# RG-LRU/HGRN2 blocks: the lambda constant, the weight splits and the row scale put elsewhere

## The chip, the cores and the metric

The kernel runs on one core of one Trainium2 chip. The metric is the device time of one execution in microseconds, as the median of several runs. Names of engines: TensorE (PE in the profile, PEld for its weight loads), VectorE (DVE), ScalarE (ACT), GpSimd (POOL), SyncE (SP, which issues the DMAs).

## The reference

A decoder trunk of two layers, 1024 tokens, width 1024, all in float32. Each layer normalises its input, projects it with one matrix w_in, and gives the columns to four head groups: A latent attention, B an RG-LRU recurrence, C stick-breaking attention, D an HGRN2 gated recurrence. Their outputs go through one projection, then a SwiGLU follows. This case concerns groups B and D:

```python
# B: RG-LRU
xc = depthwise_conv4(xb) + conv_b
rec_gate = sigmoid(blockdiag(xc, w_a) + b_a); in_gate = sigmoid(blockdiag(xc, w_x) + b_x)
log_a = -8.0 * rec_gate * softplus(-lam)
a = exp(log_a); u = sqrt(maximum(-expm1(2 * log_a), 0)) * (in_gate * xc)
y = scan(h = a * h + u) * gelu(gate)
# D: HGRN2
log_f = logaddexp(log(max(lb, 1e-30)), log1p(-lb) + log_sigmoid(fz)); key = (1 - lb) * sigmoid(-fz)
o = gated recurrence over chunks (q, key, v, log_f)
y = rmsnorm(o) * silu(g)
```

## The kernel before

Everything is kept with features on the 128 partitions and the 1024 tokens along the row. The input scale of the norm (RS, one value for each token) is not applied to the activations; each projected tile is multiplied by RS when it is read out of PSUM. A matrix product in near-full float32 is done as three products of two halves: every weight tile is split into w_hi and w_lo (w_lo = raw - w_hi), and so are the activations (u_hi, u_lo). `product` runs over eight k, and for each k three pairs of 128x512 matmuls (L217).

`group_bd` is one block and runs four times: for two layers, two pairs of heads each. Between blocks stands a barrier of all engines. In a block, eight weight tiles ("slots") of 128x1024 pass through two buffers (even and odd). Slot 1 is the q weights, slot 2 g, slot 3 v, slot 4 the conv input x, slot 5 the gate; slots 0 and 1 of a block were loaded and split ahead of it, and slots 6 and 7 are those of the next stage. SyncE loads slot n when slot n-2 is split; GpSimd splits slot n (`split_slot`, L200 w_hi and L203 w_lo) when the product of slot n-2 has ended, and multiplies g, v and gate by RS (L593) after ScalarE has copied them from PSUM (L734, L737, L742).

The order of the work on each engine is written out by hand. VectorE starts with the constants of the pair: copies L773 and L775, and then the softplus of -lambda as a chain of one-column steps (L789 to L800). Then comes f from PSUM (L802), with ScalarE's Abs, Exp and Ln in turns, the cumulative sum (L818), and `level_in(0)`, `level_in(1)`. Then q is scaled out of PSUM (L881), which frees pair 1 for slot 3. The loop over seven levels follows: `level_keys(L)` (L844, L846), `level_scores(L-1)` (two L861, which wait for the level's last chunk on TensorE), `level_in(L+2)` (L832, L833), and at L = 4 `conv` (L868 to L875). TensorE does the levels' small matmuls (L605) inside the slot products: level 0 inside slot 3 (its last chunk ahead of k = 7), levels 1 and 2 inside slot 4, levels 3 and 4 inside slot 5, level 5 behind it, and level 6 between the matmuls of the gates w_a and w_x (L648). The gates want pair 1 of PSUM free, which the read of gate does.

PSUM is used in four pairs of banks; `bank_free[p]` counts the reads that free pair p.

Of the kernel before, what the change touches and what calls it, by code (L numbers as in the profile page):

```python
# [26 lines left out]
F32 = mybir.dt.float32  # L27
# [40 lines left out]
W_LBA, W_LBC, W_LBD, W_C1, W_T0, W_T1, W_T2, W_T3, W_T4, W_N = 9, 10, 11, 12, 13, 14, 15, 16, 17, 18  # L68
# [11 lines left out]
def build(nc, x, positions, vec_table, w_in, w_uq, w_ukv, w_a, w_x, lb_logits, w_out,  # L80
# [5 lines left out]
    with ctx:  # L86
# [15 lines left out]
        lbt = fixed("lower_bound", [P, 3, 4])  # L102
# [197 lines left out]
        LW = at_r("lb_work", 73, [P, 12, 4])  # L300
        PI_ = at_r("pos_int", 76, [1, S], I32)
# [13 lines left out]
        lb_step = sem("lb_step")  # L315
        with nc.Block() as block:
# [26 lines left out]
            def _(dve):  # L343
# [3 lines left out]
                dve.wait_ge(small_loaded, 80)  # L347
# [55 lines left out]

                dve.wait_ge(x_rs, 2)
# [10 lines left out]
            def _(act):  # L415
                act.wait_ge(lb_step, 3)
# [33 lines left out]
            def _(pe):  # L450
                pe.wait_ge(small_loaded, 80)
# [51 lines left out]
        lam_part = sem("lam_part")  # L503
# [33 lines left out]
        gelu_part = sem("gelu_part")  # L537
        pool_scaled = sem("pool_scaled")
# [3 lines left out]
        la_ready = sem("la_ready")  # L542
# [9 lines left out]
        def group_bd(l, pr):  # L552
# [8 lines left out]
            with nc.Block() as block:  # L561
# [18 lines left out]
                @block.gpsimd  # L580
                def _(pool):

                    nc.gpsimd.memset(SC[:, :, :, :], 0.0).then_inc(sc_zero, 1)
                    nc.gpsimd.memset(ST[:, :, :], 0.0).then_inc(st_zero, 1)
                    nc.gpsimd.memset(XP[:, 0:3], 0.0).then_inc(st_zero, 1)

                    for n in range(2, len(slots) + 2):
                        split_slot(pool, n, n // 2, n - 2)
                        if n in (4, 5, 7):
                            t, (read, count) = {4: (bG, (bank_free[0], 2)), 5: (bV, (bank_free[1], 2)),  # L590
                                                7: (GT, (bank_free[1], 3))}[n]
                            pool.wait_ge(read, count)
                            nc.gpsimd.tensor_tensor(t[:, :], t[:, :], RS[:, :], ALU.mult).then_inc(pool_scaled, 1)  # L593

                @block.tensor
                def _(pe):
# [39 lines left out]
                    pe.wait_ge(pool_scaled, 2)  # L636
# [67 lines left out]
                def _(act):  # L704
                    exp_and_ln()

                    act.wait_ge(pair_vecs, 2)
                    nc.scalar.activation(col(W_T0), col(V_LAM), ACT.Abs).then_inc(lam_part, 1)
                    act.wait_ge(lam_part, 1)
                    nc.scalar.activation(col(W_T0), col(W_T0), ACT.Exp, scale=-1.0).then_inc(lam_part, 1)  # L710
# [6 lines left out]
                    nc.scalar.activation(bT[:, :], bT[:, :], ACT.Ln, bias=1.0).then_inc(f_soft, 1)  # L717

# [8 lines left out]
                    act.wait_ge(cum_ready, NCH)  # L727
                    nc.scalar.activation(EC[:, :], bCUM[:, :], ACT.Exp).then_inc(ec_ready, 1)
# [12 lines left out]
                    act.wait_ge(proj_done, 5)  # L741
                    nc.scalar.activation(wide(GT[:, :]), pair(1), ACT.Copy).then_inc(bank_free[1], 1)  # L742
# [6 lines left out]
                    act.wait_ge(pool_scaled, 3)  # L749
                    nc.scalar.activation(GE[:, :], GT[:, :], ACT.Square).then_inc(gelu_sq, 1)  # L750
                    nc.scalar.activation(XP[:, 0:S], bG[:, :], ACT.Sigmoid).then_inc(silu_th, 1)
                    act.wait_ge(gelu_in, 1)
                    nc.scalar.activation(GE[:, :], GE[:, :], ACT.Sigmoid, scale=2 * math.sqrt(2 / math.pi))\
                        .then_inc(gelu_th, 1)
                    act.wait_ge(la_ready, 1)
                    act.wait_ge(level_done, LEVELS)
                    nc.scalar.activation(TH[:, :], TR[:, :], ACT.Tanh).then_inc(decay_ready, 1)
                    exp_and_ln()
                    act.wait_ge(dve_step, 1)
                    nc.scalar.activation(XP[:, 0:S], TR[:, :], ACT.Exp).then_inc(decay_ready, 1)  # L760
# [7 lines left out]
                    act.wait_ge(neg_ready, 1)  # L768
                    nc.scalar.activation(TH[:, :], TH[:, :], ACT.Sqrt).then_inc(root_ready, 1)

                @block.vector
                def _(dve):
                    nc.vector.tensor_copy(pv[:, 0:PAIR_ROWS], vecs[:, bass.ds(pr * PAIR_ROWS, PAIR_ROWS)])\  # L773
                        .then_inc(pair_vecs, 1)
                    nc.vector.tensor_copy(pv[:, W_LBA:W_LBA + 3].rearrange("p (i o) -> p i o", o=1),  # L775
                                          lbt[:, :, bass.ds(l * 2 + pr, 1)]).then_inc(pair_vecs, 1)
                    dve.wait_ge(pair_vecs, 2)


                    n = 2  # L780

                    def step(ins):
                        nonlocal n
                        n += 1
                        ins.then_inc(pair_vecs, 1)
                        dve.wait_ge(pair_vecs, n)

                    nc_ts = nc.vector.tensor_scalar
                    step(nc_ts(col(W_T1), col(V_LAM), -1.0, 0.0, ALU.mult, ALU.max))  # L789
                    dve.wait_ge(lam_part, 2)  # L790
                    step(nc_ts(col(W_T2), col(W_T0), 2.0, None, ALU.add))
                    step(nc.vector.reciprocal(col(W_T2), col(W_T2)))
                    step(nc.vector.tensor_tensor(col(W_T2), col(W_T2), col(W_T0), ALU.mult))
                    step(nc.vector.tensor_tensor(col(W_T3), col(W_T2), col(W_T2), ALU.mult))
                    step(nc_ts(col(W_T4), col(W_T3), 1.0 / 17, 1.0 / 15, ALU.mult, ALU.add))
                    for term in (13, 11, 9, 7, 5, 3, 1):
                        step(nc_ts(col(W_T4), col(W_T4), col(W_T3), 1.0 / term, ALU.mult, ALU.add))
                    step(nc.vector.tensor_tensor(col(W_T4), col(W_T4), col(W_T2), ALU.mult))
                    step(nc.vector.scalar_tensor_tensor(col(W_T4), col(W_T4), 2.0, col(W_T1), ALU.mult, ALU.add))
# [83 lines left out]
                    for L in range(LEVELS):  # L883
# [3 lines left out]
                        if L + 2 < LEVELS:  # L887
                            level_in(L + 2)
# [1148 lines left out]
```

## Time and profile before

| what | value |
|---|---|
| median of 3 runs | 3028.69 us (3024.24 to 3029.8) |
| profiled execution, span | 3029.8 us, the value of the slowest of the three runs too |
| TensorE busy | 2841.3 us, 94% |
| VectorE / ScalarE / GpSimd busy | 1501.9 / 735.0 / 1143.6 us |
| mean granted TensorE clock | 0.949 of full speed |
| the four blocks of `group_bd` | from 49, 181, about 1524 and 1655 us, 122 to 132 us each |

The span is cut by barriers: setup up to 49 us, and in each layer two blocks of `group_bd`, the latents, attention and the feed-forward part. Busy time that overlaps a busier engine costs nothing by itself; what counts are the waits of the engine that is last in each stretch.

### The profile page before, as it was taken

To read this page: it belongs to the slowest core of one execution; us is meant where nothing else is said; L and a number is where in the kernel's file an instruction comes from. 1 tells how busy PE (TensorE), PEld (TensorE's weight loads), DVE (VectorE), ACT (ScalarE), POOL (GpSimd) and SP (SyncE) were. 2 spreads that over 40 slices of the span, in tenths; PEclk is the share of its full clock that TensorE was granted. 3 is DMA by queue.
4 is the path that set the end of the run, shared out by engine and by line. 5 is a ranking of instruction groups with operands and counts; after the bars stand their busy time and mean duration, and the time that the engine had idled before them with its cause. 6 is when DMAs were issued, how large, how long until landed. Compare 5 with 4: busy or idle time off the path is not lost. (4 is left out here: it accounts for less than half of the span.)

```text
span 3029.8 us, 33194 instructions
## 1 busy us (share of the span) xinstructions
PE 2841.3 (94%) x13112; PEld 2217.0 (73%) x13112; DVE 1501.9 (50%) x1745; ACT 735.0 (24%) x980; POOL 1143.6 (38%) x522
## 2 busy tenths in 40 slices
PE   7898989879999999999988899889799999999997
PEld 5666767567788888888866667566578888888886
DVE  6778248773323333332668853678522333333336
ACT  5233136562100000000223221656411000000003
POOL 3332332125544443344532323222265434434434
PEclk8899989789999999999999989788899999999999
DMA  4010210011211111111110011000212111111113
GB/s 160 15 35 8 56 25 1 0 70 36 63 49 55 56 42 48 42 42 55 70 44 21 22 29 45 8 1 0 77 49 77 47 43 42 42 48 59 52 35 111
DMA packets 201198, 134.53 MB, mean 44 GB/s; under 512 B 29346, under 2 KB 189218, under 8 KB 201123
## 3 DMA queue, kind: packets, MB, share of 16 engines
q1 hardware_dynamic: 201122, 133.49, 14.4%
q8 instruction: 51, 0.84, 0.1%
q14 instruction: 25, 0.20, 0.0%
HBM read 116.69 MB, written 16.78 MB: 44 GB/s over the span
## 5 line engine op out<-in xcount | busy, mean ns | idle before, releaser
L217 PE MATMUL ps<-u_hi,w_hi 128*128 128x512 f32 x2384 | 770.6, 405 | 58.2 <-DVE q L881 21.2
L217 PE MATMUL ps<-u_lo,w_hi 128*128 128x512 f32 x2384 | 753.7, 397 | 0.0
L217 PE MATMUL ps<-u_hi,w_lo 128*128 128x512 f32 x2384 | 753.1, 397 | 0.0
L217 PEld LDWEIGHTS ps<-u_hi,w_hi 128*128 128x128 f32 x2384 | 445.4, 190 | 172.1 <-issue 38.8
L217 PEld LDWEIGHTS ps<-u_lo,w_hi 128*128 128x128 f32 x2384 | 453.5, 190 | 106.8
L217 PEld LDWEIGHTS ps<-u_hi,w_lo 128*128 128x128 f32 x2384 | 453.1, 190 | 106.5
L1591 POOL TENSOR_TENSOR w_hi<-w_raw,ones 128x1024 fp32r<-128x1024 f32 x88 | 166.7, 1894 | 441.0 <-PE ps L217 436.5
L200 POOL TENSOR_TENSOR w_hi<-w_raw,ones 128x1024 fp32r<-128x1024 f32 (+1 forms) x62 | 118.9, 1918 | 512.9 <-PE ps L217 411.9
L1663 DVE TENSOR_TENSOR h<-ps,h 128x1024 f32<-128x1024 f32 x176 | 211.3, 1218 | 149.1 <-PE ps L217 149.1
L1648 DVE TENSOR_TENSOR hidden<-ps,hidden 128x1024 f32<-128x1024 f32 x44 | 53.9, 1225 | 434.3 <-PE ps L217 434.3
L1594 POOL TENSOR_TENSOR w_lo<-w_raw,w_hi 128x1024 fp32r<-128x1024 f32 x88 | 251.0, 2852 | 6.9
L1631 ACT ACTIVATE hidden<-hidden 128x1024 f32<-128x1024 f32 x44 | 46.7, 1061 | 740.8 <-DVE hidden L1644 740.8
L1444 POOL TENSOR_TENSOR sb_weight<-sb_z,sb_weight 128x256 f32<-128x256 f32 (+7 forms) x64 | 89.9, 1404 | 348.6 <-DVE sb_weight L1410 348.6
L1644 DVE TENSOR_TENSOR hidden<-ps,rs 128x1024 f32<-128x1024 f32 x44 | 53.9, 1224 | 314.0 <-PE ps L217 295.6
L1601 POOL TENSOR_TENSOR down_hi<-down_raw,ones 128x1024 fp32r<-128x1024 f32 x40 | 77.7, 1943 | 320.5 <-DVE h L1663 320.5
L217 PE MATMUL ps<-hidden_hi,down_hi 128*128 128x512 f32 x640 | 197.2, 389 | 0.0
L217 PE MATMUL ps<-hidden_hi,down_lo 128*128 128x512 f32 x640 | 197.2, 389 | 0.0
L217 PE MATMUL ps<-hidden_lo,down_hi 128*128 128x512 f32 x640 | 197.1, 389 | 0.0
L203 POOL TENSOR_TENSOR w_lo<-w_raw,w_hi 128x1024 fp32r<-128x1024 f32 (+1 forms) x62 | 171.2, 2761 | 4.9
L1635 ACT ACTIVATE hidden_hi<-hidden 128x1024 fp32r<-128x1024 f32 x44 | 46.8, 1063 | 518.8 <-DVE hidden L1651 518.8
L217 PEld LDWEIGHTS ps<-hidden_hi,down_hi 128*128 128x128 f32 x640 | 120.1, 188 | 25.2
L217 PEld LDWEIGHTS ps<-hidden_lo,down_hi 128*128 128x128 f32 x640 | 120.1, 188 | 25.1
(307 smaller groups left out, 3623.4 us busy)
## 6 DMA issues: line engine op xcount, KB each, us to landing
w_raw<-w_in SPq DMA_DIRECT2D x44, 512.0 KB, 3.8
w_raw<-w_gate SPq DMA_DIRECT2D x44, 512.0 KB, 3.7
w_raw<-w_up SPq DMA_DIRECT2D x44, 512.0 KB, 3.8
down_raw<-w_down SPq DMA_DIRECT2D x44, 512.0 KB, 5.1
h_spill<-h SPq DMA_DIRECT2D x24, 512.0 KB, 2.6
w_raw<-w_out SPq DMA_DIRECT2D x16, 512.0 KB, 3.4
h<-h_spill SPq DMA_DIRECT2D x16, 512.0 KB, 6.8
x_in<-x SPq DMA_DIRECT2D x8, 512.0 KB, 7.1
```

Of the source, the lines that this page charges most:

```text
L200: nc.gpsimd.tensor_tensor(whi[i][:, 0:width], raw[i][:, 0:width], ones[:, 0:1].broadcast_to([P, width]), ALU.mult).then_inc(hi_split, 1)
L203: nc.gpsimd.tensor_tensor(wlo[i][:, 0:width], raw[i][:, 0:width], whi[i][:, 0:width].bitcast(F32), ALU.subtract).then_inc(slot_split, 1)
L217: last = nc.tensor.matmul(ps[:, bank0 + half, :], a, b[:, half * HALF:(half + 1) * HALF], start=(k == order[0] and n == 0), stop=(k == ord ...
L1444: nc.gpsimd.tensor_tensor(RW[i % 2][:, 0:n], ZS[i % 2][:, 0:n], RW[i % 2][:, 0:n], ALU.subtract).then_inc(lw_ready, 1)
L1591: nc.gpsimd.tensor_tensor(whi[q % 2][:, :], raw[q % 2][:, :], ones[:, 0:1].broadcast_to([P, 1024]), ALU.mult).then_inc(hi_split, 1)
L1594: nc.gpsimd.tensor_tensor(wlo[q % 2][:, :], raw[q % 2][:, :], whi[q % 2][:, :].bitcast(F32), ALU.subtract).then_inc(slot_split, 1)
L1601: nc.gpsimd.tensor_tensor(DHI[t][:, :], DRAW[t][:, :], ones[:, 0:1].broadcast_to([P, 1024]), ALU.mult).then_inc(down_hi, 1)
L1631: nc.scalar.activation(HT[t][:, :], HT[t][:, :], ACT.Silu).then_inc(silu_done, 1)
L1635: nc.scalar.activation(HIDH[b][:, t, :], HT[t][:, :], ACT.Copy).then_inc(hid_hi, 1)
L1644: nc.vector.tensor_tensor(wide(HT[t][:, :]), pair(pg), wide(RS[:, :]), ALU.mult)\
L1648: nc.vector.tensor_tensor(wide(HT[t][:, :]), pair(pu), wide(HT[t][:, :]), ALU.mult)\
L1663: nc.vector.tensor_tensor(wide(h[:, m, :]), pair(p), wide(h[:, m, :]), ALU.add)\
```

## The change

Four things are done, nearly all in `group_bd`:

1. The constant -8 softplus(-lambda) is computed once in setup for both layers and pairs (a new DMA of 2 KB, two ScalarE and 23 VectorE instructions of 4 columns), and stored as a fourth row of `lbt`. A block copies the constants on ScalarE.
2. `split_slot` on GpSimd is gone from the block: `slot_hi` on ScalarE and `slot_lo` on VectorE take its place, each at a place in its engine's order.
3. The reads of g, v and gate from PSUM are VectorE multiplications by RS; ScalarE's copies and GpSimd's multiplications are gone.
4. Around the decay and gelu: the multiplication of rec_gate by the constant goes into the `scale` of Tanh and Exp, the square of the decay goes to ScalarE, gelu's scale and product are one instruction, and the maximum with zero is a Relu on ScalarE ahead of Sqrt.

```diff
 # setup, @block.sync
+    sp.dma_start(LV[:, 0, :], lam[:, :]).then_inc(small_loaded, 16)
...
 # setup, @block.vector, behind the angles and ahead of the wait on x_rs
+    dve.wait_ge(lam_soft, 2)
+    lam_next(nc.vector.tensor_scalar(v(5), v(0), -1.0, 0.0, ALU.mult, ALU.max))
...
+    for term in (13, 11, 9, 7, 5, 3, 1):
+        lam_next(nc.vector.tensor_tensor(v(4), v(4), v(3), ALU.mult))
+        lam_next(nc.vector.tensor_scalar(v(4), v(4), 1.0 / term, None, ALU.add))
...
+    lam_next(nc.vector.tensor_scalar(lbt[:, 3, :], v(4), -LRU_C, None, ALU.mult))
...
 # group_bd
 @block.scalar
+    def slot_hi(n):
+        i = n % 2
+        act.wait_ge(raw_loaded[i], 16 * (n // 2))
+        if n > 2:
+            act.wait_ge(proj_done, n - 2)
+        nc.scalar.activation(whi[i][:, :], raw[i][:, :], ACT.Copy).then_inc(hi_split, 1)
...
+    slot_hi(2)        # behind the first Ln
...
+    slot_hi(3)        # behind key
     for L in range(LEVELS):
         act.wait_ge(e_in, 2 * (L + 1))
         nc.scalar.activation(LE[L % 2][:, :], LE[L % 2][:, :], ACT.Exp).then_inc(e_ready, 1)
-        if L == 1:
-            act.wait_ge(proj_done, 2)
-            nc.scalar.activation(wide(bG[:, :]), pair(0), ACT.Copy).then_inc(bank_free[0], 1)
-        if L == 3:
-            act.wait_ge(proj_done, 3)
-            nc.scalar.activation(wide(bV[:, :]), pair(1), ACT.Copy).then_inc(bank_free[1], 1)
+        if L in (1, 3, 5):
+            slot_hi({1: 4, 3: 5, 5: 6}[L])
...
-    act.wait_ge(proj_done, 5)
-    nc.scalar.activation(wide(GT[:, :]), pair(1), ACT.Copy).then_inc(bank_free[1], 1)
...
+    nc.scalar.activation(XC[:, :], XP[:, 0:S], ACT.Square).then_inc(decay_sq, 1)
+    slot_hi(7)
...
     act.wait_ge(neg_ready, 1)
+    nc.scalar.activation(TH[:, :], TH[:, :], ACT.Relu, scale=-1.0).then_inc(root_ready, 1)
+    act.wait_ge(root_ready, 1)
     nc.scalar.activation(TH[:, :], TH[:, :], ACT.Sqrt).then_inc(root_ready, 1)

 @block.vector
+    def slot_lo(n):
+        i = n % 2
+        dve.wait_ge(hi_split, n - 1)
+        nc.vector.tensor_tensor(wlo[i][:, :], raw[i][:, :], whi[i][:, :].bitcast(F32),
+                                ALU.subtract).then_inc(slot_split, 1)
-    step(nc_ts(col(W_T1), col(V_LAM), -1.0, 0.0, ALU.mult, ALU.max))
...
-    step(nc_ts(col(W_C1), col(W_T4), -LRU_C, None, ALU.mult))
...
     nc.vector.tensor_scalar(bM[:, :], bB[:, :], col(W_LBC), col(W_LBA), ALU.add, ALU.max)
     dve.wait_ge(logf_ready, 1)
+    slot_lo(2)
...
     nc.vector.tensor_tensor(wide(bQ[:, :]), pair(1), wide(RS[:, :]), ALU.mult).then_inc(bank_free[1], 1)
+    slot_lo(3)
     for L in range(LEVELS):
         level_keys(L)
         if L >= 1:
             level_scores(L - 1)
         if L + 2 < LEVELS:
             level_in(L + 2)
+        if L == 1:
+            dve.wait_ge(proj_done, 2)
+            nc.vector.tensor_tensor(wide(bG[:, :]), pair(0), wide(RS[:, :]), ALU.mult).then_inc(bank_free[0], 1)
+            slot_lo(4)
+        if L == 3:
+            dve.wait_ge(proj_done, 3)
+            nc.vector.tensor_tensor(wide(bV[:, :]), pair(1), wide(RS[:, :]), ALU.mult).then_inc(bank_free[1], 1)
+            slot_lo(5)
         if L == 4:
             conv()
+        if L == 5:
+            slot_lo(6)
     nc.vector.tensor_tensor(chunks(bF), ..., ALU.subtract).then_inc(kx2_ready, 1)
+    dve.wait_ge(proj_done, 5)
+    nc.vector.tensor_tensor(wide(GT[:, :]), pair(1), wide(RS[:, :]), ALU.mult).then_inc(bank_free[1], 1)
...
+    slot_lo(7)        # behind y_d, ahead of the product with the root
     dve.wait_ge(root_ready, 2)
     nc.vector.tensor_tensor(TI[:, :], TI[:, :], TH[:, :], ALU.mult).then_inc(dve_step, 1)

 @block.gpsimd
-    for n in range(2, len(slots) + 2):
-        split_slot(pool, n, n // 2, n - 2)
-        if n in (4, 5, 7):
...
-            nc.gpsimd.tensor_tensor(t[:, :], t[:, :], RS[:, :], ALU.mult).then_inc(pool_scaled, 1)

 @block.tensor
-    pe.wait_ge(pool_scaled, 2)
+    pe.wait_ge(bank_free[1], 2)
```

## Rows read from the trace of the kernel before

**Rows 1.** The page: busy time, share and instructions of each engine.
```profile
PE 2841.3 (94%) x13112; PEld 2217.0 (73%) x13112; DVE 1501.9 (50%) x1745; ACT 735.0 (24%) x980; POOL 1143.6 (38%) x522
```

**Rows 2.** The page's costliest groups: busy, mean | idle before, releaser.
```profile
L217 PE MATMUL ps<-u_hi,w_hi 128*128 128x512 f32 x2384 | 770.6, 405 | 58.2 <-DVE q L881 21.2
```

**Rows 3.** Timeline of TensorE, first block: start, us, instruction [idle before <-releaser].
```profile
81.28 1.22 PE L217 MATMUL ps<-u_hi,w_hi 128*128 128x512 f32 x2 [7.56 <-DVE q L881]
...
98.15 0.66 PE L605 MATMUL ps<-q_level,log_f 64*128 64x64 f32 x8
...
115.76 0.66 PE L605 MATMUL ps<-q_level,log_f 64*128 64x64 f32 x8
...
133.19 2.00 PE L605 MATMUL ps<-q_level,log_f 64*128 64x64 f32 x32
...
138.34 2.38 PE L648 MATMUL ps<-x_conv,w_a_blocks 128*128 128x512 f32 x4 [2.12 <-ACT gate L742]
...
142.12 2.07 PE L648 MATMUL ps<-x_conv,w_x_blocks 128*128 128x512 f32 x2
...
147.60 1.12 PE L605 MATMUL ps<-q_level,log_sig 64*128 64x64 f32 x8
```

**Rows 4.** Timeline of VectorE, start of the first block.
```profile
55.95 1.71 DVE L797 TENSOR_SCALAR pair_vectors<-pair_vectors 128x1 f32<-128x1 f32 x7
...
58.63 1.22 DVE L802 TENSOR_TENSOR f<-ps,rs 128x1024 f32<-128x1024 f32 x1
...
80.01 1.21 DVE L881 TENSOR_TENSOR q<-ps,rs 128x1024 f32<-128x1024 f32 x1
```

**Rows 5.** Timeline of ScalarE, first block.
```profile
59.88 1.06 ACT L713 ACTIVATE soft<-f 128x1024 f32<-128x1024 f32 x1 [7.18 <-DVE f L802]
```

**Rows 6.** Timeline of VectorE, two instructions of level_keys.
```profile
103.61 3.40 DVE L846 TENSOR_TENSOR log_sig<-key,f 128x1024 f32<-128x1024 f32 x1
...
109.94 1.23 DVE L846 TENSOR_TENSOR log_f<-key,soft 128x1024 f32<-128x1024 f32 x1
```

**Rows 7.** Timeline of GpSimd, one multiplication by RS.
```profile
103.10 2.83 POOL L593 TENSOR_TENSOR v<-v,rs 128x1024 f32<-128x1024 f32 x1
```

**Rows 8.** Timeline of VectorE, first block, 96 to 175 us.
```profile
96.68 1.35 DVE L861 COPY_PREDICATED scores<-level_mask,ps 128x512 f32<-128x512 uint8 x2 [8.41 <-PE ps L605]
...
122.97 1.31 DVE L861 COPY_PREDICATED scores<-level_mask,ps 128x512 f32<-128x512 uint8 x2 [0.52 <-PE ps L605]
...
133.05 1.30 DVE L861 COPY_PREDICATED scores<-level_mask,ps 128x512 f32<-128x512 uint8 x2
...
138.96 2.45 DVE L861 COPY_PREDICATED scores<-level_mask,ps 128x512 f32<-128x512 uint8 x2
141.21 1.25 DVE L895 TENSOR_TENSOR f<-cum 128x1024 f32<-128x1024 f32 x1
...
174.29 1.22 DVE L962 TENSOR_TENSOR in_gate<-in_gate,tanh_log_a 128x1024 f32<-128x1024 f32 x1
```

**Rows 9.** Timeline of VectorE in setup.
```profile
29.36 1.23 DVE L405 TENSOR_TENSOR rs_diagonal<-x_mean_sq,constants 128x1024 f32<-128x1024 f32 x1 [3.49 <-ACT x_mean_sq L435]
30.51 9.65 DVE L267 SCALAR_TENSOR_TENSOR u_lo<-h,vectors,u_hi 128x1024 fp32r<-128x1024 f32 x8
```

**Rows 10.** Timeline of TensorE, start of slot 3 in the second block.
```profile
206.99 0.72 PE L217 MATMUL ps<-u_hi,w_hi 128*128 128x512 f32 x2 [1.90 <-DVE q L881]
...
211.52 0.66 PE L605 MATMUL ps<-q_level,log_sig 64*128 64x64 f32 x8
```

**Rows 11.** Timeline of TensorE, gate phase of the second block.
```profile
263.88 1.96 PE L648 MATMUL ps<-x_conv,w_a_blocks 128*128 128x512 f32 x4 [2.12 <-ACT gate L742]
...
269.51 0.66 PE L605 MATMUL ps<-q_level,log_sig 64*128 64x64 f32 x8
```

**Rows 12.** Windows of the third block: busy of each engine, PEclk, DMA share, GB/s.
```profile
1615.00:1617.00 2.00, 2.00 (x6) 0.50 (x5) 2.00 (x3) 0.00 (x0) 1.52 (x1) 0.50 0.00 0
...
1619.00:1621.00 2.00, 2.00 (x17) 1.18 (x18) 1.11 (x1) 1.14 (x2) 0.00 (x0) 1.00 0.00 0
```

More of the change, by code:

```diff
@@ L77, with build @@
 PI_BELOW = 3.1415925
-def build(nc, x, positions, vec_table, w_in, w_uq, w_ukv, w_a, w_x, lb_logits, w_out,
+def build(nc, x, positions, vec_table, w_in, w_uq, w_ukv, w_a, w_x, lb_logits, lam, w_out,
           w_gate, w_up, w_down, consts, level_masks, out):
@@ L101, in build @@
         vecs = fixed("vectors", [P, V_ROWS])
-        lbt = fixed("lower_bound", [P, 3, 4])
+        lbt = fixed("lower_bound", [P, 4, 4])
         pv = fixed("pair_vectors", [P, W_N])
@@ L300, in build @@
         LW = at_r("lb_work", 73, [P, 12, 4])
+        LV = at_r("lam_work", 74, [P, 6, 4])
         PI_ = at_r("pos_int", 76, [1, S], I32)
@@ L315, in build @@
         lb_step = sem("lb_step")
+        lam_soft = sem("lam_soft")
+        lam_step = sem("lam_step")
         with nc.Block() as block:
@@ L402, in _, with lam_next @@
                 turn(nc.vector.tensor_scalar(AN[:, :], AN[:, :], PI_BELOW, -PI_BELOW, ALU.min, ALU.max))
+                c = 0
+                def lam_next(ins):
+                    nonlocal c
+                    c += 1
+                    ins.then_inc(lam_step, 1)
+                    dve.wait_ge(lam_step, c)
+                v = lambda i: LV[:, i, :]
+                dve.wait_ge(lam_soft, 2)
+                lam_next(nc.vector.tensor_scalar(v(5), v(0), -1.0, 0.0, ALU.mult, ALU.max))
+                lam_next(nc.vector.tensor_scalar(v(2), v(1), 2.0, None, ALU.add))
+                lam_next(nc.vector.reciprocal(v(2), v(2)))
+                lam_next(nc.vector.tensor_tensor(v(2), v(2), v(1), ALU.mult))
+                lam_next(nc.vector.tensor_tensor(v(3), v(2), v(2), ALU.mult))
+                lam_next(nc.vector.tensor_scalar(v(4), v(3), 1.0 / 17, 1.0 / 15, ALU.mult, ALU.add))
+                for term in (13, 11, 9, 7, 5, 3, 1):
+                    lam_next(nc.vector.tensor_tensor(v(4), v(4), v(3), ALU.mult))
+                    lam_next(nc.vector.tensor_scalar(v(4), v(4), 1.0 / term, None, ALU.add))
+                lam_next(nc.vector.tensor_tensor(v(4), v(4), v(2), ALU.mult))
+                lam_next(nc.vector.scalar_tensor_tensor(v(4), v(4), 2.0, v(5), ALU.mult, ALU.add))
+                lam_next(nc.vector.tensor_scalar(lbt[:, 3, :], v(4), -LRU_C, None, ALU.mult))
                 dve.wait_ge(x_rs, 2)
@@ L415, in _ @@
             def _(act):
+                act.wait_ge(small_loaded, 96)
+                nc.scalar.activation(LV[:, 1, :], LV[:, 0, :], ACT.Abs).then_inc(lam_soft, 1)
+                act.wait_ge(lam_soft, 1)
+                nc.scalar.activation(LV[:, 1, :], LV[:, 1, :], ACT.Exp, scale=-1.0).then_inc(lam_soft, 1)
                 act.wait_ge(lb_step, 3)
@@ L704, in _ @@
                 def _(act):
+                    def slot_hi(n):
[4 more added lines that the diff above has]
+                        nc.scalar.activation(whi[i][:, :], raw[i][:, :], ACT.Copy).then_inc(hi_split, 1)
                     exp_and_ln()
+                    nc.scalar.activation(pv[:, 0:PAIR_ROWS], vecs[:, bass.ds(pr * PAIR_ROWS, PAIR_ROWS)], ACT.Copy)\
+                        .then_inc(pair_vecs, 1)
+                    nc.scalar.activation(pv[:, W_LBA:W_LBA + 4].rearrange("p (i o) -> p i o", o=1),
+                                         lbt[:, :, bass.ds(l * 2 + pr, 1)], ACT.Copy).then_inc(pair_vecs, 1)
                     act.wait_ge(pair_vecs, 2)
-                    nc.scalar.activation(col(W_T0), col(V_LAM), ACT.Abs).then_inc(lam_part, 1)
-                    act.wait_ge(lam_part, 1)
-                    nc.scalar.activation(col(W_T0), col(W_T0), ACT.Exp, scale=-1.0).then_inc(lam_part, 1)
                     act.wait_ge(bank_free[0], 1)
@@ L888, in _ @@
                             level_in(L + 2)
+                        if L == 1:
+                            dve.wait_ge(proj_done, 2)
+                            nc.vector.tensor_tensor(wide(bG[:, :]), pair(0), wide(RS[:, :]), ALU.mult)\
+                                .then_inc(bank_free[0], 1)
+                            slot_lo(4)
+                        if L == 3:
+                            dve.wait_ge(proj_done, 3)
+                            nc.vector.tensor_tensor(wide(bV[:, :]), pair(1), wide(RS[:, :]), ALU.mult)\
+                                .then_inc(bank_free[1], 1)
+                            slot_lo(5)
                         if L == 4:
                             conv()
+                        if L == 5:
+                            slot_lo(6)
                     cum = chunks(bCUM)
@@ L896, in _ @@
                                             ALU.subtract).then_inc(kx2_ready, 1)
+                    dve.wait_ge(proj_done, 5)
+                    nc.vector.tensor_tensor(wide(GT[:, :]), pair(1), wide(RS[:, :]), ALU.mult)\
+                        .then_inc(bank_free[1], 1)
                     dve.wait_ge(ec_ready, 1)
```

83 lines of the change are left out of this document (27 added, 56 removed).

## The prediction, made before the changed kernel was timed

> **What bounds the kernel now.** I read the page first: TensorE is busy 94% of the span, VectorE half of it, GpSimd 38% [rows 1]. So only work that makes TensorE wait is worth time. The costliest group of instructions shows where it waits: of 58.2 us of idle time ahead of the first product of a slot, 21.2 us end with one VectorE instruction, the scaling of q at L881 [rows 2]. From then on I read the first of the four recurrence blocks (49 to 181 us) in order of time, VectorE and ScalarE beside TensorE, then the second (181 to 303 us). In the first, TensorE waits 7.6 us for q, runs three slot products behind each other without a wait (slot 3 from 81.28, slot 4 from 98.15, slot 5 from 115.76 to 133.19), then waits 2.1 us for ScalarE's gate copy, and from 133 us on it shares the path with VectorE [rows 3]. The same pattern stands in all four blocks; only the q wait differs (1.9 us in the second).
>
> **The start of a block.** Today VectorE first works out the lambda constant: steps of 0.2 us each, 7 of them 1.71 us [rows 4], and scales f at 58.63, 9 us after the start; q is scaled at 80.01. In the changed kernel f is scaled at once; ScalarE starts its Abs some 2 us after the block's start (a table load of 1.3 and two copies of 0.2), at 51.4 instead of 59.88 [rows 5]. Between this Abs and the end of q lie 21.3 us today, of which VectorE lost about 7 to GpSimd: an L846 with a GpSimd multiplication beside it takes 3.40, one alone 1.23 [rows 6, 7], and this stretch has four such instructions, slowed by 1.3 to 2.1 each. With GpSimd's splits gone and none of the new instructions on the chain (ScalarE's split of slot 2 fits before its second Abs, VectorE's while ScalarE does its second softplus), q is done at about 51.4 + 21.3 - 7 = 66, and slot 3 is split at 68. TensorE ends slot 2 at 73.6 by its own work. All the waits on q go: 21.2 us. With the wait goes what it does to the clock: slot 3 takes 16.9 us (81.28 to 98.15); slot 5 takes 17.4 with eight level chunks more, at 0.66 for two [rows 3], so slot 3 would be 14.8 at full clock. That is 2.1, taken as 2.0 in each block. Term: -21.2 - 8.0 = **-29.2**. The cover for the moved work is 5.5 us of slack (68 against 73.6); if it were gone, each us late costs one per block.
>
> **The reads of g and v, and the splits of slots 4 and 5.** Before, ScalarE and GpSimd did these early, in their own queues. Now they stand in VectorE's queue behind level_scores(0) and level_in(3), and for slot 5 behind level_scores(2) and level_in(5). level_scores can't start before the last chunk of a level, and that chunk is issued with the last k of the slot product: L861 starts at 96.68 and slot 4 at 98.15 [rows 3, 8]; slot 5 shows the same 1.5, as do the other blocks. So VectorE begins 1.5 us before TensorE wants the next slot, and then has to do the two score copies (1.2), level_in (1.2), the scaled read (1.2) and the subtraction (1.2, by u_lo, eight in 9.65 [rows 9]): 4.9 us. TensorE waits 3.4 us, at two places in each of four blocks. And the clock: after a wait of only 1.90 us in the second block the six pairs from 206.99 to 211.52 take 4.5 us, where 0.47 each would be 2.8 [rows 10]. That is 1.7 more; I take 1.6. The bounds are nothing (the clock holds) and 2.1 (as after the wait of 7.6). Term: 8 x (3.4 + 1.6) = **+40.0**. The four waits of 0.2 on a slowed L846 go: **-0.8**.
>
> **The gate product.** It wants pair 1 free; today that is ScalarE's copy, and TensorE starts at 138.34, 5.15 behind the end of slot 5 (133.19) [rows 3]. Now it is a VectorE read behind slot_lo(6), level_keys(6), level_scores(5) and the L895 subtraction. From level_scores(3) at 122.97: 10.1 to level_scores(4) at 133.05, 1.2 for it, 1.2 for slot_lo(6), 1.8 for the keys (0.6 and 1.2 without GpSimd), 2.25 for level_scores(5) (138.96 to 141.21), 1.2 for L895 and 1.2 for the read [rows 8]: 19.0, so 141.9, or 8.7 behind the end of slot 5. It is 3.55 later: 4 x 3.55 = **+14.2**. The wait grows to 5.7 us, so the gate phase begins at the lower of the clock's two levels (1.2 of 2.4 GHz). Today this phase (first w_a matmul to the last level 6 matmul) takes 10.4 us in the first block, in which the clock fell, and 6.3 in the second, in which it held [rows 3, 11]; in the third and fourth 7.9 and 10.9. If the clock is low throughout, the w_a matmuls too cost what the w_x ones do, 2.07 for two [rows 3], so 12.2 in each: +13. If it comes back after some 4 us, as in the third (0.50 at 1615 to 1617 us, 1.00 from 1619) [rows 12], 8.2 in each: -3. I take 9.5: **+2.5**.
>
> **The tail of a block.** The states and the product that reads them are paced by TensorE, so the two VectorE instructions dropped ahead of them (0.7 each) give nothing, nor does the square, which ScalarE takes in idle time. After the Exp of the norm, ScalarE now does the Relu before the Sqrt: one more pass of 1.06 [rows 5] on the chain that ends with Sqrt and, behind it, the product at 174.29 [rows 8]; the last slot_lo(7) ends at about the same time. 4 x 1.15 = **+4.6**. The page "ScalarE: Activation LUTs" of the Trainium skill (section Rules for kernel authors) says that max and relu belong on VectorE, not ScalarE. By it the edit is a loss too; with the 0.69 that VectorE's own pass takes in the trace, but off this chain, the term would be 0 if the Relu were left there.
>
> **Setup.** One more small DMA ahead of the others (0.4 in SP's queue) and 23 small VectorE steps of 0.2: 4.6 us. VectorE was idle for 3.49 ahead of L405 [rows 9]; the chain ends about 1.6 late with the DMA's share, and u_lo, for which TensorE waits, with it: **+1.6**. Bounds 0.4 (all covered) and 5.
>
> Other edits cost nothing: the loads of slots 6 and 7 are issued later (behind slot_lo(4) and slot_lo(5), with the gate weights behind them in SP's queue), but still some 20 us ahead of their use; the pool's scaling of g, v and gate is gone, and its three reads cost the same on VectorE as plain reads.
>
> **Sum:** -29.2 + 40.0 - 0.8 + 14.2 + 2.5 + 4.6 + 1.6 = +32.9 us, against the profiled span of 3029.8, which is also the time of the slowest of the three runs and 1.1 above their median. So 3028.7 + 33 = **3062 us**, 1.1% slower.
>
> **Rivals.**
> *The clock holds through the short waits.* For it: the clock held across 2.1 us ahead of the second block's gate product [rows 11]. Against: it fell after 1.90 [rows 10]. Without the eight 1.6 it gives 33 - 13 = +20: 3049.
> *The gate phase stays at the low clock.* For it: the first block's 10.4. Against: it came back in the third. +13 instead of +2.5: 3072.
> *Faster: no new wait at slots 4 and 5.* VectorE idles 8.4 us ahead of the score copies at 96.68 [rows 8], and has GpSimd's slowing to lose: 2.2 us in the instruction shown [rows 6, 7], some 28 over all of the first block. If TensorE's level signal left VectorE 4.9 us or more before a slot ends, the term of 40 would vanish: 33 - 40 = -7: 3022. It decides from there: with waits of under about 0.8 us and no loss of clock the kernel is level. The page "GPSIMD Engine Reference" of the Trainium skill (section Key points) says that GpSimd contends with VectorE instructions that have two SBUF inputs; the trace agrees (3.40 against 1.23). Against this rival: the idle time ends with that very signal, 1.5 us before the slot's end, and the queue order is fixed.
> *No effect.* The q wait and the new waits cancel, with waits of some 3 us at five places rather than twelve: 3029. Nothing in the rows speaks for it.
>
> **Chances and range.** Forecast 0.50; clock holds 0.21; gate phase low 0.17; faster 0.07; no effect 0.05. The forecast by itself spans 3054 to 3068. The range reaches over the two clock cases, whose far ends are +9 (no clock lost anywhere, fast gate phase in all blocks: 3038) and +52 (3081): 3042 to 3079. A change of 0.2% is about what can be told here. Faster 0.07, same 0.05, slower 0.88.
>
> **What would show it.** In the changed profile: no wait on q at L881 (now 21.2); TensorE waiting about 3.4 us eight times on slot 4 and 5's w_lo; 5 to 6 us ahead of the gate product, ended by the scaled read of gate; L846 at 1.2 everywhere; the recurrence blocks longer by 5 to 11 us each, the second and third most; all else the same. I am wrong if slots 3, 4 and 5 still follow each other without a gap, or if level_scores(0) ends well ahead of slot 3's last product.

## The result, and the profile after

The changed kernel takes 3083.9 us (median of four runs, 3075.4 to 3100.3), the kernel before, run beside it, 3028.7 (3024.2 to 3029.8): a ratio of 1.0200, 95% interval 1.0165 to 1.0235. It is slower by 55 us. The direction was as forecast, the size was not: 3062 was forecast, the range ended at 3079, and the median lies 5 us beyond it. The profiled execution took 3086.35 us with a span of 3084.3, so 54.5 more than the span of before; the terms below are measured against this 54.5.

The page's first part and its costliest group after the change, answering to [rows 1, 2]:

```profile
PE 2868.8 (93%) x13112; PEld 2238.6 (73%) x13112; DVE 1419.5 (46%) x1716; ACT 754.3 (24%) x1002; POOL 993.8 (32%) x462
...
L217 PE MATMUL ps<-u_hi,w_hi 128*128 128x512 f32 x2384 | 780.2, 409 | 43.1 <-PEq L161 19.9
```

GpSimd and VectorE have less to do than before, and the idle time ahead of the products no longer ends with q. Yet the product instructions themselves are dearer: this one group is busy for 780.2 us instead of 770.6. Work that was not changed took longer, which is what a lower clock looks like on the page. The mean granted clock fell with it, from 0.949 to 0.940. The list of TensorE's waits names where it now stops:

```profile
PE ps L626 <- issue: 26.7, 8, 3.4
PE ps L669 <- DVE gate L926: 22.6, 4, 5.6
PE ps L217 <- PEq L161: 19.9, 5, 4.6
...
PE ps L688 <- DVE log_f L937: 9.3, 4, 2.3
```

Columns are the total, the number of waits and the longest. Eight waits of 3.4 and four of 5.6: the two new waits that the prediction priced at 3.4 and, for the gate, at 5.7. The first carries the name "issue" and no engine, so its cause has to be read from VectorE's timeline of the first block:

```profile
65.94 1.22 DVE L895 TENSOR_TENSOR q<-ps,rs 128x1024 f32<-128x1024 f32 x1
...
87.28 1.35 DVE L875 COPY_PREDICATED scores<-level_mask,ps 128x512 f32<-128x512 uint8 x2 [14.20 <-PE ps L626]
88.53 0.67 DVE L846 TENSOR_TENSOR soft<-cum 128x512 f32<-128x512 f32 x1
89.12 0.68 DVE L847 TENSOR_TENSOR soft<-cum 128x512 f32<-128x512 f32 x1
89.73 1.21 DVE L906 TENSOR_TENSOR g<-ps,rs 128x1024 f32<-128x1024 f32 x1
90.86 1.21 DVE L811 TENSOR_TENSOR w_lo<-w_raw,w_hi 128x1024 fp32r<-128x1024 f32 x1
...
147.95 1.25 DVE L922 TENSOR_TENSOR f<-cum 128x1024 f32<-128x1024 f32 x1
149.12 1.21 DVE L926 TENSOR_TENSOR gate<-ps,rs 128x1024 f32<-128x1024 f32 x1
```

q is done at 67, where 66 was worked out, instead of at 81 [rows 4]. After the keys of level 1 VectorE idles for 14.2 us until TensorE's level matmuls release the score copies at 87.28, and then does the copies, level_in, the read and the split in a row, up to 92.1. TensorE begins slot 4 at 92.17. The read of g and the split have nothing to do with the scores; they stand behind them.

TensorE in the same block, answering to [rows 3], and slot 4 of the second:

```profile
92.17 1.12 PE L626 MATMUL ps<-q_level,log_f 64*128 64x64 f32 x8 [3.35 <-issue]
93.22 1.22 PE L217 MATMUL ps<-u_hi,w_hi 128*128 128x512 f32 x2
...
107.80 1.12 PE L626 MATMUL ps<-q_level,log_sig 64*128 64x64 f32 x8
108.85 0.74 PE L217 MATMUL ps<-u_hi,w_hi 128*128 128x512 f32 x2
...
110.46 0.66 PE L626 MATMUL ps<-q_level,log_sig 64*128 64x64 f32 x8
...
141.81 2.00 PE L626 MATMUL ps<-q_level,log_f 64*128 64x64 f32 x32
...
150.48 3.34 PE L669 MATMUL ps<-x_conv,w_a_blocks 128*128 128x512 f32 x4 [5.63 <-DVE gate L926]
...
235.35 1.12 PE L626 MATMUL ps<-q_level,log_f 64*128 64x64 f32 x8 [3.35 <-issue]
...
254.89 1.02 PE L626 MATMUL ps<-q_level,log_sig 64*128 64x64 f32 x8
255.84 0.73 PE L217 MATMUL ps<-u_hi,w_hi 128*128 128x512 f32 x2
...
265.20 0.66 PE L626 MATMUL ps<-q_level,log_f 64*128 64x64 f32 x8 [3.34 <-issue]
265.80 1.13 PE L217 MATMUL ps<-u_hi,w_hi 128*128 128x512 f32 x2
...
269.51 0.73 PE L217 MATMUL ps<-u_hi,w_hi 128*128 128x512 f32 x2
```

A level chunk pair takes 1.12 at 92.17 and still 1.12 at 107.80, and 0.66 from 110.46 on: the clock was at the lower of its two levels for over 15 us behind a wait of 3.35. In slot 4 of the second block it was for 20 (235.35 to 255.84), but in slot 5 of the same block, which begins with level matmuls too and behind the same wait, only for 3.7 (265.80 to 269.51). Windows over whole slots say the same (length, busy of PE, PEld, VectorE, ScalarE and GpSimd, granted clock, DMA share, GB/s). After, slots 4 and 5 of the first two blocks:

```profile
92.17:117.02 24.85, 24.85 (x112) 17.71 (x112) 7.40 (x11) 1.06 (x1) 0.00 (x0) 0.66 0.09 22
120.36:141.81 21.45, 21.42 (x112) 15.41 (x112) 11.71 (x14) 1.06 (x1) 0.00 (x0) 0.79 0.12 28
...
235.35:261.86 26.51, 26.50 (x112) 18.84 (x112) 7.41 (x11) 1.06 (x1) 0.00 (x0) 0.62 0.08 20
265.20:284.19 18.99, 18.95 (x113) 13.63 (x113) 11.72 (x14) 1.06 (x1) 0.00 (x0) 0.91 0.12 31
```

Before, slot 4 of the first block took 17.61 (98.15 to 115.76) and slot 5 17.43 (115.76 to 133.19) [rows 3]. The eight slots after take 24.85, 21.45, 26.51, 18.99, 23.1, 19.0, 26.5 and 19.0, together 179.4; eight slots of before at the mean of 17.52 are 140.2. That is 39 us of lost clock, where the prediction had 8 x 1.6 = 12.8.

### The profile page after: what moved, and what is told of

Read it like the earlier page. It is cut to its first block and busy times, and to the rows that moved or that the text cites. A ratio compares the mean times of both kernels' runs of the same rounds, so it can differ in the third digit from the quotient of the medians.

```text
span 3084.3 us, 33141 instructions
## 1 busy us (share of the span) xinstructions
PE 2868.8 (93%) x13112; PEld 2238.6 (73%) x13112; DVE 1419.5 (46%) x1716; ACT 754.3 (24%) x1002; POOL 993.8 (32%) x462
## 5 line engine op out<-in xcount | busy, mean ns | idle before, releaser
L217 PE MATMUL ps<-u_hi,w_hi 128*128 128x512 f32 x2384 | 780.2, 409 | 43.1 <-PEq L161 19.9
L217 PE MATMUL ps<-u_lo,w_hi 128*128 128x512 f32 x2384 | 761.9, 401 | 0.0
L217 PE MATMUL ps<-u_hi,w_lo 128*128 128x512 f32 x2384 | 761.3, 401 | 0.0
L200 POOL TENSOR_TENSOR w_hi<-w_raw,ones 128x1024 fp32r<-128x1024 f32 (+1 forms) x38 | 70.3, 1849 | 524.6 <-DMA w_raw<-w_in 299.3
L217 PEld LDWEIGHTS ps<-hidden_hi,down_lo 128*128 128x128 f32 x640 | 120.1, 188 | 25.0
```

Source lines behind the costliest of these rows:

```text
L200: nc.gpsimd.tensor_tensor(whi[i][:, 0:width], raw[i][:, 0:width], ones[:, 0:1].broadcast_to([P, width]), ALU.mult).then_inc(hi_split, 1)
L217: last = nc.tensor.matmul(ps[:, bank0 + half, :], a, b[:, half * HALF:(half + 1) * HALF], start=(k == order[0] and n == 0), stop=(k == ord ...
```

## The experiments

Ten kernels were run in three batches, each batch beside the kernel before, which took 3024.2 us beside runs 1, 2, 3 and 6, 3021.5 beside runs 5, 8 and 9, and 3022.4 beside runs 4, 7 and 10: 5 to 7 less than beside the changed kernel. So a difference of medians from the changed kernel's 3083.9 is unsure by that much, and the ratios say it better. Lines starting with + and - are against the kernel named.

**1. The lambda constant alone** (against the kernel before: the chain in setup, nothing else moved).

```
+ (setup) lam_next(nc.vector.tensor_scalar(lbt[:, 3, :], v(4), -LRU_C, None, ALU.mult))
+ (block) nc.scalar.activation(pv[:, 0:PAIR_ROWS], vecs[...], ACT.Copy)
- (block) step(nc_ts(col(W_C1), col(W_T4), -LRU_C, None, ALU.mult))   # and the 20 steps before it
```

> The kernel before with part 1 of the change alone: the lambda constant in setup, the pair's constants copied on ScalarE; splits and scalings of g, v, gate stay where they were. Theory (the wait on q comes from the constant's chain at the start of the block): f is scaled 7 to 9 us earlier, q is done within 1 to 2 us of the end of slot 2, and the 21.2 us of waits on q fall to under 5: 3000 to 3008. Rival (VectorE is slowed by GpSimd so much that only taking the splits off GpSimd frees q): the waits on q stay above 10 us: 3015 or more.

Measured: 2997.0 us (2995.1 to 3005.1), ratio 0.9916 (0.9891 to 0.9942). The waits on q are gone. By the medians (3024.2 for the kernel before, run beside it) that is 27 us less, by the interval 18 to 33; 29.2 was predicted for the start of a block. The median is 3 us below the range expected. GpSimd still splits here, so the constant's chain alone made the waits. This part is a gain of 0.8%, and the loss lies in the other parts.

**2. The reads of g and v early** (against the changed kernel: within one level of the loop, the scaled read and the weight split stand ahead of the scores).

```
                         level_keys(L)
+                        if L == 1: ... bG read; slot_lo(4)
+                        if L == 3: ... bV read; slot_lo(5)
                         if L >= 1: level_scores(L - 1)
                         if L + 2 < LEVELS: level_in(L + 2)
-                        if L == 1: ... bG read; slot_lo(4)
-                        if L == 3: ... bV read; slot_lo(5)
```

> The changed kernel with the reads of g and v and the splits of slots 4 and 5 put ahead of the score copies of the same level. Theory (the eight waits of 3.35 and the long low clock behind them are made by these two places in VectorE's queue alone): the waits go (-27) and slots 4 and 5 take 17.4 again (-39): about 3018 against 3084. Rival A (VectorE has too much work in slots 4 and 5 once it has the splits): waits come back elsewhere in these slots, 3040 or more. Rival B (the clock is low in slot 4 for another reason than the wait): only the 27 go, about 3057.

Measured: 3016.5 us (3012.9 to 3024.8, ten runs), ratio 0.9974 (0.9954 to 0.9993). All eight waits are gone, and slot 4 of the first block is back at full clock:

```profile
87.60:104.94 17.34, 17.34 (x114) 12.59 (x113) 10.78 (x15) 3.07 (x3) 0.00 (x0) 1.00 0.13 33
```

The order of four instructions in one queue is worth 67 us: 27 of waiting and 39 of clock. The work itself, on the same engine, costs nothing in these slots: all eight take 17.4 or less.

**3. The gate product's read early too** (against run 2: the read of gate stands ahead of slot_lo(6), behind the scores of level 4).

```
                         if L == 5:
+                            dve.wait_ge(proj_done, 5); ... GT read, bank_free[1]
                             slot_lo(6)
```

> As reads_early, with the read of gate put behind level_scores(4), ahead of slot_lo(6), in place of behind the L922 subtraction. Theory: the four waits of 5.6 ahead of the gate product go, the phase starts at full clock, and VectorE, which then reaches its product with the decayed key about 11 us behind slot 5, is next: some 5 us a block, 2992 to 3002. Rival (the gate phase is bound by VectorE's keys of level 6 in any case): no more than 5 us below reads_early.

Measured: 3000.9 us (2985.2 to 3004.8), ratio 0.9899 (0.9854 to 0.9944). The gate wait is gone; part of it passes to the next operand, log_sig, whose four waits grow to 9.9 in all.

**4. The gate read early alone** (against the changed kernel; the reads of g and v stay late).

> The changed kernel with the gate product's PSUM read and the weight split of the last product alone issued early on VectorE; the reads of bG and bV stay late. The eight waits ahead of slots 4 and 5 and their low clock stay (slot 4 about 25 long, slot 5 about 19 to 21). Theory (the gate wait is the read's place in VectorE's queue and independent of the other two): the four waits of 5.6 ahead of the gate product go, or shrink to 2.5 at another operand as they did where all reads were early; 13 to 22 less than the changed kernel's, 3062 to 3071. Rival (the gate wait comes from VectorE's total work at the end of the phase): less than 5 gained, 3079 to 3084.

Measured: 3070.4 us (3061.8 to 3074.4), ratio 1.0158 (1.0125 to 1.0192), 14 us below the changed kernel in the medians; the two intervals overlap. The eight waits stay as they were, the gate wait is gone, and what takes its place is small:

```profile
PE ps L626 <- issue: 28.3, 11, 3.4
...
PE ps L681 <- DVE log_sig L934: 9.5, 4, 2.5
...
PE ps L688 <- DVE log_f L937: 6.1, 4, 1.7
```

Waits on gate, log_sig and log_f were 22.6, 5.6 and 9.3 after the change, 37.5 together, and are 15.6 here. So the two new waits are independent of each other, and each is set by a read's place in the queue. Of the eight slots behind the waits of 3.3 seven take from 19.0 to 26.5, and one, slot 5 of the fourth block, loses nothing at all:

```profile
1758.33:1775.75 17.42, 17.42 (x112) 12.58 (x112) 11.68 (x14) 1.06 (x1) 0.00 (x0) 1.00 0.13 34
```

**5. GpSimd splits again** (against the changed kernel: slot_hi(2) to slot_hi(7) and slot_lo(2) to slot_lo(7) are left out, and GpSimd splits the slots as before; the scaled reads stay on VectorE, late).

```
+                    for n in range(2, len(slots) + 2):
+                        split_slot(pool, n, n // 2, n - 2)
```

> The changed kernel with part 2 alone undone: GpSimd splits slots 2 to 7 again, ScalarE and VectorE don't; the scaled reads of g, v and gate stay on VectorE at their late places. Theory (what makes TensorE wait at slots 4 and 5 is that these pairs are read behind the score copies; which engine splits matters less): VectorE has 1.2 us less to do there, but GpSimd's subtraction of slot 5 or 6 runs at just that moment and slows the second half of level_in from 0.7 to 2.4, so the waits stay at 3.5 to 4 us, eight times, and the time stays between 3070 and 3095. Rival (the splits on VectorE are the cause): the waits fall under 1 us and the time under 3040.

Measured: 3100.7 us (3080.8 to 3105.1), ratio 1.0238 (1.0191 to 1.0285). TensorE waits for the reads of g and v four times each, 3.9 at most, and 7.5 for gate. The time lies 6 us above the range expected, and far from the rival's. So the splits on VectorE alone are not the cause: without them the waits are longer. The run does not show what the reads alone would cost without any splits beside them, for it trades the 1.2 us of the split for GpSimd's slowing of VectorE, 1.7 here:

```profile
92.07 0.67 DVE L842 TENSOR_TENSOR soft<-cum 128x512 f32<-128x512 f32 x1
92.66 2.38 DVE L843 TENSOR_TENSOR soft<-cum 128x512 f32<-128x512 f32 x1
94.97 1.21 DVE L901 TENSOR_TENSOR g<-ps,rs 128x1024 f32<-128x1024 f32 x1
```

```profile
92.51 1.98 POOL L200 TENSOR_TENSOR w_hi<-w_raw,ones 128x1024 fp32r<-128x1024 f32 x1 [15.02 <-PE ps L217]
94.57 2.69 POOL L203 TENSOR_TENSOR w_lo<-w_raw,w_hi 128x1024 fp32r<-128x1024 f32 x1
```

The second of two equal instructions takes 2.38 instead of 0.67 when a GpSimd split lies beside it; the scaled read, with one operand from PSUM, keeps its 1.21. The page "GPSIMD Engine Reference" of the Trainium skill (section Key points) names contention of GpSimd with VectorE instructions that have two SBUF inputs; the trace agrees on both rows.

**6. Level chunks not beside the first products** (against the changed kernel: in slots 4 and 5 the eight chunks that stood two beside each of k = 0 to 3 stand four beside k = 2 and four beside k = 3; the same work in another order, the waits untouched).

```
+    first = {2: (0, 1, 2, 3), 3: (4, 5, 6, 7)}
-    for chunk in (2 * (k % 4), 2 * (k % 4) + 1):
+    for chunk in first.get(k, ()) if k < 4 else (2 * (k % 4), 2 * (k % 4) + 1):
         level(L + k // 4, chunk)
```

> The changed kernel with its eight waits of 3.35 left in, but the chunks of level 1 (in slot 4) and level 3 (in slot 5) issued four each at k = 2 and k = 3, none at k = 0 and 1. Theory (the clock comes back soon after a wait when slot products run alone and stays low while level matmuls stand between them): the clock is back within some 4 us after each wait, slots 4 and 5 take about 19 instead of 19 to 26.5: 25 to 30 us less, about 3056. Rival (the length of the wait, or chance, sets how long the clock stays low): slot 4 takes 23 to 26 us as before, 3075 to 3090.

Measured: 3052.0 us (3045.9 to 3070.0), ratio 1.0101 (1.0049 to 1.0152), 32 us below the changed kernel by the medians and 30 by the ratios. The waits stand, and the clock behind them comes back soon, as here in slot 4 of the second block:

```profile
PE ps L217 <- DVE w_lo L812: 27.1, 8, 3.4
```

```profile
222.35 1.19 PE L217 MATMUL ps<-u_hi,w_hi 128*128 128x512 f32 x2 [3.40 <-DVE w_lo L812]
...
225.05 0.95 PE L217 MATMUL ps<-u_hi,w_hi 128*128 128x512 f32 x2
225.84 0.62 PE L217 MATMUL ps<-u_lo,w_hi 128*128 128x512 f32 x2
...
226.85 1.11 PE L626 MATMUL ps<-q_level,log_f 64*128 64x64 f32 x16
```

Two products take 1.19 right behind the wait and 0.62 from 225.84 on: 3.5 us, where the same place of the changed kernel needed 20 (235.35 to 255.84). The sixteen level matmuls that follow at 226.85 take 1.11, as long as eight do at the lower clock, so they run at the full one and do not bring it down. The eight slots take 17.0, 17.0, 18.5, 19.4, 19.6, 18.5, 18.5 and 19.4: 11.9 over eight times 17.0, instead of 39. The two of 17.0, those of the first block, lost nothing, for behind the same wait the clock did not fall at all:

```profile
111.23:128.17 16.94, 16.94 (x112) 12.48 (x112) 11.64 (x14) 1.06 (x1) 0.00 (x0) 1.00 0.15 36
```

The row of waits also names what the changed kernel's page called "issue": with no level matmul in front, the same eight waits are put down to slot_lo's w_lo.

**7. One product group alone** (as run 6, with the chunks three beside k = 1, three beside k = 2 and two beside k = 3).

> The changed kernel, with the eight level chunks of levels 1 and 3 placed three beside k = 1, three beside k = 2 and two beside k = 3 of the slot behind them, none beside k = 0 (the changed kernel: two beside each k). The waits ahead of slots 4 and 5 stay at 3.3 to 3.4. Theory (the clock stays low after a wait while 64-column level matmuls stand between the slot products, and comes back where the products run alone): one k alone, about 4.3 long, is nearly the 5.4 behind which the clock was back in the run with two k alone, so the loss over the eight slots lies between the 11.9 of that run and the 39.3 of the changed kernel, nearer the first: 12 to 25, a time of 3052 to 3070. Rival (only the order of the level chunks and their own waits on copies mattered, not what follows the wait at once): 3080 or so, slots 4 still at 23 to 26.

Measured: 3062.2 us (3056.1 to 3075.3), ratio 1.0141 (1.0104 to 1.0179), between the two; its interval overlaps both that of run 6 and that of the changed kernel (1.0165 to 1.0235), so by time alone it can be told from neither. The waits are 3.4 as before, and the slots show that the loss isn't a smooth price:

```profile
90.76:108.04 17.28, 17.27 (x112) 12.48 (x112) 7.38 (x11) 1.06 (x1) 0.00 (x0) 1.00 0.12 31
...
229.09:247.85 18.76, 18.76 (x112) 13.46 (x112) 7.36 (x11) 1.06 (x1) 0.00 (x0) 0.91 0.11 28
...
1584.89:1609.45 24.56, 24.56 (x112) 17.57 (x112) 7.35 (x11) 1.06 (x1) 0.00 (x0) 0.67 0.09 22
```

Four of the eight slots take 17.28 to 17.32, two 18.8, and two 23.3 and 24.6, behind waits of 3.38 to 3.40 each: 16.4 over eight times 17.28, within the 12 to 25 expected. In the four of 17.3 the granted clock is 1.00 throughout.

**8. The maximum back on VectorE** (against run 3: VectorE takes the maximum ahead of ScalarE's Sqrt, no Relu).

> gate_early with the maximum with zero on VectorE again, as it was in the kernel before, in place of ScalarE's Relu. Theory (the Relu lies on the chain behind the last Exp): Sqrt ends 1.05 us earlier, but slot_lo(7) then holds the product by itself, so the product starts no more than 0.3 us earlier, and the four blocks give 1 us in all: no difference that these runs can tell. Rival (Relu alone is the cost): 4 to 5 us.

Measured: 2996.0 us (2991.7 to 3007.3), ratio 0.9905 (0.9876 to 0.9934): no difference from run 3 that can be told. Sqrt ends about 1 us earlier, but in the first block the time from the start of the addition that makes o (cum<-ps,v; L967 here, L969 in run 3) to the start of the block's last instruction (y_b) is 14.28 instead of 14.26, because slot_lo(7) stands ahead of the product that waits for Sqrt. The page "ScalarE: Activation LUTs" of the Trainium skill (section Rules for kernel authors) puts max and relu on VectorE; no run here shows the speed in bf16 that it speaks of, in float32 the pass takes 0.69 on VectorE (L975) against 1.04 on ScalarE (L801 of run 3), and the move alone changed no time that can be told, as another instruction was as late.

**9. The last splits out of the way as well** (against run 8: slot_lo(7) ahead of the wait for o_done, where VectorE idles, and slot_lo(6) behind the product of the key with its decay).

```
                     dve.wait_ge(od_ready, 1)
+                    slot_lo(7)
                     dve.wait_ge(o_done, 1)
```

> relu_back with slot_lo(7) put ahead of VectorE's wait for o (where it idles 1.7 us) and slot_lo(6) behind the product with the decayed key. Theory: the end of a block comes 1.2 us earlier, the gate phase's wait for that product falls from 2.5 to 1.4 us: about 2.3 us a block, 9 us below gate_early, some 2990. Rival (the block's end is set elsewhere, by TensorE's slot 6): under 3 us.

Measured: 2989.0 us (2981.0 to 2989.7), ratio 0.9878 (0.9847 to 0.9910). The same stretch takes 13.20, 1.08 less, and TensorE's waits at the ends of the blocks (L161) fall from 19.8 to 15.3. The other half of what was expected did not come: of the waits in the gate phase those on log_sig fall from 9.9 to 7.6 (2.5 to 1.9 each), but those on log_f, next in the queue, grow from 6.2 to 12.5.

**10. One split and one product later** (against run 9: slot_lo(6) ahead of the wait for the state update, q times key behind the copy of the transposed key).

> The version with the early reads and the moved tail splits, with the split of slot 6 issued directly ahead of the wait for the state update, and the product of q and key moved behind the copy of the transposed key. Theory (at a block's end VectorE's queue sets when TensorE goes on, by the 1.2 of a split each): about 1.1 less per block, four blocks, so 4 less than the 2989.0 of the version it starts from: about 2985, ratio to the kernel before 0.985 to 0.988. Rival (the wait only passes to the next operand of the queue): no change, 2989, ratio 0.988.

Measured: 2989.7 us (2978.2 to 2999.3, six runs), ratio 0.9881 (0.9851 to 0.9912). The waits of TensorE did shrink; in run 9 those on log_f and log_sig are

```profile
PE ps L688 <- DVE log_f L935: 12.5, 4, 3.4
...
PE ps L681 <- DVE log_sig L931: 7.6, 4, 1.9
```

and here

```profile
PE ps L688 <- DVE log_f L933: 9.3, 4, 2.3
...
PE ps L681 <- DVE log_sig L930: 5.7, 4, 1.4
```

5.1 us less waiting, and no less time: neither the expected 4 us nor their absence can be told where runs of one kernel spread over 21 us. Runs 9 and 10 are the best versions found, 1.2% faster than the kernel before.

## Why the prediction was right in its direction and wrong in its size

The steps, each as predicted and as the profile after has it (us, over the four blocks):

| step | predicted | measured |
|---|---|---|
| waits on q | -21.2 | -21.2, none left |
| clock behind them (slot 3) | -8.0 | -6.7; slot 3 takes 15.1 in every block, was 16.9, 16.7, 17.1, 16.5 |
| eight waits at slots 4 and 5 | +27.2 | +26.7 |
| clock behind these | +12.8 | +39.3 |
| waits of 0.2 on a slowed L846 | -0.8 | gone, and inside the row above (slot 4 of before holds them); the instruction takes 1.22 throughout |
| gate product starts later | +14.2 | +14.1; 8.67 behind slot 5's end, was 5.15 |
| clock of the gate phase | +2.5 | -3.7; 7.7, 8.1, 7.8, 8.1 against 10.4, 6.3, 7.9, 10.9 |
| tail of a block | +4.6 | +4.6; 14.27 against 13.12 |
| setup | +1.6 | 0 |
| sum | +32.9 | +53.1, of a difference of 54.5 |

**The step that failed** is the price of the clock behind a short wait, "I take 1.6", with bounds of 0 and 2.1. Measured: 39.3 / 8 = 4.9 on the mean, from 1.5 to 9.0. The mechanism was right (the wait lowers the clock) and its place too; the size was taken from slot 3 [rows 10], and slot 3 isn't like slots 4 and 5. In slot 3 the products stand alone at first; the first level matmul comes at 211.52, 4.5 us behind the wait [rows 10]. Slots 4 and 5 begin with level matmuls and have them beside every product group [rows 3]. The bounds had been taken from slot 3 as well, so the range inherited the error. That the difference matters is what runs 6 and 7 show: the same waits and the same work, with the level matmuls moved behind two product groups or one, gave 11.9 and 16.4 instead of 39.3. Runs 4 and 5, in which the level matmuls stand as in the changed kernel behind waits of 3.3 and 3.9, gave about 42 and 38 against the same 17.52 a slot, so the 39.3 is no chance of one execution.

But the order moves only the mean, from 4.9 a place (24 places of the changed kernel and of runs 4 and 5) to 1.8 (16 places of runs 6 and 7). At a single place it does not decide: with the level matmuls first, slot 5 lost 1.5 in three of four blocks of the changed kernel, just the 1.6 of the prediction, and nothing in one of run 4; with products first, two slots of run 7 lost 6 and 7. So the step had a second fault: it took what one wait had cost at one place as the price of eight. What sets the loss at a single place is not shown.

With this price alone the sum would have been 32.9 + 26.5 = 59.4; the gate phase (6.2 less), setup (1.6 less) and slot 3 (1.3 more) are the other large differences, and they nearly bring it to the 53.1 of the table. The far ends that the prediction gives its range, +9 and +52, come out of its own terms as +7 and +51 (the second with setup at its bound of 5); neither reaches the measured time.

**The start of a block** went as worked out. Run 1 shows this part alone: 27 us of gain (18 to 33) where 29.2 was predicted, though with GpSimd's splits still in place, and so without the 7 us that the prediction took from their going.

**The reads behind the scores** were the right cause. Run 2 removes the waits by order alone, run 5 keeps them without VectorE's splits. The rival that VectorE might have time before the slot ends was the right question with the wrong condition: VectorE idled for 14.2 us ahead of the scores (87.28), and the reads could have used it, but the order of the queue didn't let them.

**The gate phase** came out with the other sign, but that the change shortened it is not shown: in run 1, where the gate part and its four waits of 2.1 are those of before, the phase takes 6.3, 7.8, 8.0 and 7.8, 5.7 less than in the profile of before and 1.9 less than after the change. In the changed kernel the clock came back in all four blocks, as in the third block of before [rows 12], also where the wait had grown to 5.6; the four w_a matmuls take 3.34 to 3.75 and the w_x pairs behind them 1.13. The rival "the gate phase stays at the low clock" was borne out by no block, and "the clock holds through the short waits" by none of the eight slots of the changed kernel, of which the shortest takes 19.0 (it did hold at one place of run 4). After a wait of 5.6 the gate phase lost less than slot 4 did after one of 3.35; what follows the wait differs there too, 512-column w_a products alone.

**The tail** came to 1.15 in the first block, and TensorE's waits at the ends of the blocks grew by 4.7 in all (L161: 15.2, then 19.9), but not for the reason given alone: removing the Relu gains nothing (run 8) until the split of slot 7 is moved as well (run 9). Two things were equally late, and the prediction had named both.

**Setup**: the 4.6 us of small steps fit, because VectorE reaches them at 24.84, 1.0 earlier than it was through with the work ahead of them before; L432 starts at 29.45 where L405 started at 29.36 [rows 9], and setup ends at 48.7 in both.

Taken from barrier to barrier, the four blocks are 10.6, 20.7, 11.1 and 10.7 us longer, 53.1 together (5 to 11 each was expected, the second and third most). The 1.4 us that are left of the 54.5 lie in the stages that the change does not touch, which differ by up to 4.6 us either way between these two profiles. What stays open is why, behind equal waits with equal work, some slots lose nothing and some 7 us (run 7) or 9 (run 4).

## What to carry to other kernels

When work moves into another engine's queue, ask not only how long it takes but what it stands behind: here a read that was ready for 14 us waited for the scores, and putting it ahead of them turned a loss of 2% into a gain of 0.3%. Price the clock behind a new wait from several stretches with the same mix of matmuls as the one that will follow it, not from a single neighbour whose mix differs, and give it a wide range: here 0 to 9 us a place. A change of several parts is worth timing by parts: one of these was worth -0.8%, hidden under the +2.9% (1.0200 / 0.9916) of the rest.

## What the runs showed of the hardware beyond what was expected

- A wait of 3.4 us ahead of small matmuls cost more in clock than in waiting: 39 us against 27 over eight places. With 64-column matmuls among the products from the start, the clock was down for 15 us (92.17 to 107.80) and 20 us (235.35 to 255.84), but once for only 3.7 (265.80 to 269.51); where products ran alone first it was back after 3.5 us (222.35 to 225.84) or had never fallen (111.23 to 128.17), and the same small matmuls then ran at the full clock. The mean loss was 4.9 us a place against 1.8.
- A wait of 3.34 us was once followed by no fall of the clock (run 4, 1758.33), while one of 1.90 was [rows 10].
- A GpSimd instruction beside VectorE stretched a 0.67 us subtraction to 2.38 and left a read from PSUM at 1.21.
- The kernel before alone spread over 24 us in fifteen runs (3014.9 to 3038.7) beside runs 1, 2, 3 and 6, where its four beside the changed kernel lay within 5.6; differences of a few us between single medians can't be told.
